# Stick-breaking attention: the scores of four heads stay in four PSUM banks, and the sums of kept logarithms are added onto them by pairs of heads

## The reference

```
z = einsum('bhqd,bhkd->bhqk', q_blk, kh) * scale
mask = (key_pos[None, :] < q_pos[:, None]) & key_valid[None, :]
log_beta = where(mask, log_sigmoid(z), -inf)
log_keep = where(mask, log_sigmoid(-z), 0.0)
later = cumsum(log_keep, axis=3, reverse=True) - log_keep
a = exp(log_beta + later)
out = einsum('bhqk,bhkd->bhqd', a, vh)
```

## Time and profile before

| | us |
|---|---|
| median of 3 runs | 1073.82 |
| lowest and highest | 1071.89, 1075.95 |
| the profiled execution | 1075.32 |
| its span, first to last instruction | 1073.5 |
| PE busy | 1043.0 (97%) |
| DVE, ACT, POOL busy | 596.4, 513.9, 150.2 |
| mean granted clock of TensorE | 0.991 |

### The profile page before, as it was taken

How to read it: one execution, slowest core, us unless ns; L and a number is a source line. 1 busy time by engine, 2 the same in 40 slices (tenths; PEclk the granted TensorE clock), 3 DMA queues, 4 the chain that set the end, 5 groups by cost and what they waited for, 6 DMA issues and landing times.

```text
span 1073.5 us, 20398 instructions
## 1 busy us (share of the span) xinstructions
PE 1043.0 (97%) x7936; PEld 970.1 (90%) x7936; DVE 596.4 (56%) x837; ACT 513.9 (48%) x811; POOL 150.2 (14%) x140
## 2 busy tenths in 40 slices
PE   8899999999989999999989999999999899999998
PEld 5899878889977999999969998788899879999997
DVE  8456345436676555554465564554458666666543
ACT  5442454456445544453455334534563565454542
POOL 2000000000354221110130000000006332212011
PEclk9899999999999999999999999999999999999999
DMA  5673422334442455555525533233354425555551
GB/s 168 228 235 100 147 78 81 118 118 158 145 158 90 157 182 170 169 173 187 168 86 171 183 110 127 79 118 94 128 173 157 157 91 184 195 182 176 195 190 40
DMA packets 156042, 157.46 MB, mean 147 GB/s; under 512 B 6851, under 2 KB 154542, under 8 KB 155598
## 3 DMA queue, kind: packets, MB, share of 16 engines
q1 hardware_dynamic: 155118, 153.17, 44.2%
q10 hardware_dynamic: 672, 3.37, 0.9%
q0 software_dynamic: 192, 0.07, 0.0%
HBM read 155.55 MB, written 1.05 MB: 146 GB/s over the span
## 4 chain that ended last, share of the span: by engine, by line
PE 87%; DVE 8%; ACT 1%; issue 1%; DMA 1%; ACTq 0%; DVEq 0%
PE banks L548 26%; PE banks L550 25%; PE banks L549 25%; DVE sub L1237 2%; DVE xl L1474 2%; DVE term L1481 1%; PE banks L744 1%; DVE sq L1228 1%; PE banks L746 1%; PE banks L573 1%; PE banks L656 1%; DVE lo L1219 1%; DMA raw<-in_w_in 1%; PE banks L772 1%; ACT hi L916 1%
## 5 line engine op out<-in xcount | busy, mean ns | idle before, releaser
L548 PE MATMUL banks<-xh,hi 128*128 128x272 f32 (+1 forms) x1680 | 492.5, 293 | 16.1 <-DVE xl L1252 4.8
L550 PE MATMUL banks<-xh,lo 128*128 128x272 f32 (+1 forms) x1680 | 482.9, 287 | 0.0
L549 PE MATMUL banks<-xl,hi 128*128 128x272 f32 (+1 forms) x1680 | 481.5, 287 | 0.0
L1219 DVE TENSOR_TENSOR lo<-raw,hi 128x1024 fp32r<-128x1024 f32 (+1 forms) x292 | 350.8, 1206 | 182.5 <-ACT hi L916 181.3
L916 ACT ACTIVATE hi<-raw 128x1024 fp32r<-128x1024 f32 (+1 forms) x292 | 302.9, 1041 | 130.1 <-PE banks L550 100.6
L548 PEld LDWEIGHTS banks<-xh,hi 128*128 128x128 f32 x1680 | 319.2, 190 | 31.0 <-issue 14.7
L549 PEld LDWEIGHTS banks<-xl,hi 128*128 128x128 f32 x1680 | 319.0, 190 | 0.7
L550 PEld LDWEIGHTS banks<-xh,lo 128*128 128x128 f32 x1680 | 319.3, 190 | 0.0
L1603 POOL TENSOR_TENSOR half<-term 128x544 f32<-128x544 f32 (+1 forms) x14 | 31.1, 2222 | 518.3 <-DVE term L1481 518.0
L550 PE MATMUL banks<-ah,lo 128*128 128x272 f32 (+1 forms) x352 | 100.4, 285 | 0.0
L548 PE MATMUL banks<-ah,hi 128*128 128x272 f32 (+1 forms) x352 | 100.1, 284 | 0.0
(11 more groups left out here) (239 smaller groups left out, 1094.8 us busy)
## 6 DMA issues: line engine op xcount, KB each, us to landing
raw<-in_w_in SPq DMA_DIRECT2D x60, 1024.0 KB, 5.0
raw<-in_ffn_w_gate SPq DMA_DIRECT2D x22, 1024.0 KB, 5.1
raw<-in_ffn_w_up SPq DMA_DIRECT2D x22, 1024.0 KB, 5.1
raw<-in_ffn_w_down SPq DMA_DIRECT2D x16, 1024.0 KB, 5.2
raw<-in_w_branch SPq DMA_DIRECT2D x8, 1024.0 KB, 5.3
raw<-in_w_out SPq DMA_DIRECT2D x8, 1024.0 KB, 5.2
raw<-in_ffn_w_down SPq DMA_DIRECT2D x8, 768.0 KB, 4.4
const<-in_consts ACTq DMA_DIRECT2D x2, 1042.5 KB, 5.3
```

What stands on the lines that cost most here:

```text
L548: mm(dst, wh, mh, start=start, stop=False)
L549: mm(dst, wh, ml, start=False, stop=False)
L550: return mm(dst, wl, mh, start=False, stop=stop)
L1219: tt(lo[g % 2][:, 0:k, c:c + P], raw[g % 2][:, 0:k, c:c + P], hi[g % 2][:, 0:k, c:c + P].bitcast(F32), ALU.subtract).then_inc(lo_ready, 1)
```

## The change

The score banks are now four, one for each head: `z_banks` = `sc[0]`, `sc[1]`, `ex`, `e0`. All scores are computed once, at the start, and stay there. `sb_exponent` works on a pair of heads and adds the sums onto the scores without computing them again; the sums for the meta keys go onto `k0`, where `sb_scores0` has left its scores. In a score bank only the first matmul has `start`. The softplus, `sb_keep` and `sb_mask` read the bank of their head, `sb_mask0` reads `k0`. The steps are put in another order: both `sb_scores` together; `sb_soft` 1 and `sb_keep` 1 ahead of group `mo`; `sb_soft` 2 and `sb_keep` 2 behind it; `sb_exponent` 0 behind `sbv`; `sb_soft` 3 and `sb_keep` 3 behind that; the second `sb_exponent` behind logit half 0. `gla_scores0` waits in addition for `e0_free`, and `gla_scores` for `ex_free` of all heads. Eight semaphores that existed once for each layer exist once, with a target of l + 1.

```
-           ("sb_scores0",), ("sb_scores", 0), ("sb_soft0",), ("sb_keep0",), ("sb_soft", 0), ("sb_keep", 0),
-           ("group", "mo"), ("sb_exponent", 0), ("sb_soft", 1), ("sb_mask", 0), ("sb_p", 0), ("sb_keep", 1),
-           ("group", "sbv"), ("rest", "sbv"), ("sb_exponent", 1), ("sb_scores", 1)]
+           ("sb_scores0",), ("sb_scores", 0), ("sb_scores", 1), ("sb_soft0",), ("sb_keep0",), ("sb_soft", 0), ("sb_keep", 0),
+           ("sb_soft", 1), ("sb_keep", 1), ("group", "mo"), ("sb_soft", 2), ("sb_keep", 2), ("group", "sbv"), ("rest", "sbv"),
+           ("sb_exponent", 0), ("sb_soft", 3), ("sb_keep", 3)]
...
-    0: [("sb_soft", 2), ("sb_mask", 1), ("sb_p", 1), ("sb_keep", 2)],
-    1: [("sb_soft", 3), ("sb_mask", 2), ("sb_p", 2), ("sb_keep", 3)],
-    2: [("gla_soft",), ("sb_mask", 3), ("sb_mask0",), ("sb_p", 3), ("sb_p0",)],
+    0: [("sb_mask", 0), ("sb_p", 0), ("sb_mask", 1), ("sb_p", 1)],
+    1: [("gla_soft",), ("sb_mask", 2), ("sb_p", 2)],
+    2: [("sb_mask", 3), ("sb_mask0",), ("sb_p", 3), ("sb_p0",)],
...
-    0: [("sb_exponent", 2)],
-    1: [("sb_exponent", 3)],
+    0: [("sb_exponent", 1)],
...
+        z_banks = [*sc, ex, e0]
...
-            def sb_exponent(l, h):
-
-                qs, ks, i, rows = M["sbq"], M["sbk"], h // 2, head_rows[h]
-                keep = M["pt"]
+            def sb_scores(l, i):
+
+                qs, ks = M["sbq"], M["sbk"]
                 pe.wait_ge(rot_free[l], 4)
-                pe.wait_ge(sb_keep0[l], 1)
-                pe.wait_ge(sb_keep[l], h + 1)
-                mm(e0[quad[h], 0:T], ks[rows, i, 0:32], qs[rows, i, :], start=True, stop=False)
-                mm(e0[quad[h], 0:T], cut["negtri0"][quad[h], :], M["pt0"][quad[h], :], start=False, stop=False)
-                mm(e0[quad[h], KB1:T], cut["negones"][:, 0:32], keep[:, h, 0:256], start=False, stop=False)
-                last0 = mm(e0[quad[h], KB2:T], cut["negones"][:, 0:32], keep[:, h, 256:SCW], start=False, stop=True)
-                if h == HEADS - 1:
+                for h in (2 * i, 2 * i + 1):
+                    mm(z_banks[h][:, 0:256], ks[head_rows[h], i, KB1:KB2], qs[head_rows[h], i, KB1:], start=True, stop=False)
+                for h in (2 * i, 2 * i + 1):
+                    mm(z_banks[h][:, 256:SCW], ks[head_rows[h], i, KB2:], qs[head_rows[h], i, KB2:], start=False, stop=True).then_inc(sc_ready[l], 1)
+
+            def sb_exponent(l, i):
+
+                keep, heads = M["pt"], (2 * i, 2 * i + 1)
+                pe.wait_ge(sb_keep0, l + 1)
+                pe.wait_ge(sb_keep[l], 2 * i + 2)
+                for h in heads:
+                    mm(k0[quad[h], 0:T], cut["negtri0"][quad[h], :], M["pt0"][quad[h], :], start=False, stop=False, skip_group_check=True)
+                for h in heads:
+                    mm(k0[quad[h], KB1:T], cut["negones"][:, 0:32], keep[:, h, 0:256], start=False, stop=False, skip_group_check=True)
+                for h in heads:
+                    last0 = mm(k0[quad[h], KB2:T], cut["negones"][:, 0:32], keep[:, h, 256:SCW], start=False, stop=True, skip_group_check=True)
+                if i:
                     last0.then_inc(e0_ready[l], 1)
-                if h:
-                    pe.wait_ge(ex_free[l], h)
-                mm(ex[:, 0:256], ks[rows, i, KB1:KB2], qs[rows, i, KB1:], start=True, stop=False)
-                mm(ex[:, 0:256], cut["negtri"], keep[:, h, 0:256], start=False, stop=False)
-                mm(ex[:, 128:256], cut["negones"], keep[:, h, 256:SCW], start=False, stop=True)
-                mm(ex[:, 256:SCW], ks[rows, i, KB2:], qs[rows, i, KB2:], start=True, stop=False)
-                mm(ex[:, 256:SCW], cut["negtri"], keep[:, h, 256:SCW], start=False, stop=True).then_inc(ex_ready[l], 1)
+                for h in heads:
+                    mm(z_banks[h][:, 0:256], cut["negtri"], keep[:, h, 0:256], start=False, stop=False, skip_group_check=True)
+                    mm(z_banks[h][:, 128:256], cut["negones"], keep[:, h, 256:SCW], start=False, stop=False, skip_group_check=True)
+                    mm(z_banks[h][:, 256:SCW], cut["negtri"], keep[:, h, 256:SCW], start=False, stop=True, skip_group_check=True).then_inc(ex_ready[l], 1)
 
             def gla_scores0(l):
                 d = open_scores0(l, GLA)
+                pe.wait_ge(e0_free[l], 1)
...
             def gla_scores(l, i):
+                pe.wait_ge(ex_free[l], HEADS)
...
             def sb_soft_(l, h):
-                softplus_part(M["sb2"][:, h % 2, :], sc[h % 2][:, 0:SCW], sb_soft[l], 3 * (h + 1), (sc_ready[l], h + 1))
+                if h >= 2:
+                    act.wait_ge(sc_free[l], h - 1)
+                softplus_part(M["sb2"][:, h % 2, :], z_banks[h][:, 0:SCW], sb_soft[l], 3 * (h + 1), (sc_ready[l], h + 1))
```

More of the change, by code:

```diff
@@ L384, in build @@
         sq_first = sem("sq_first")
+        mo_ready, den_abs, hrstd_ready, hlog_ready, sb_p0, sb_keep0, den_ready, ml_em = (
+            sem(n) for n in ("mo_ready", "den_abs", "hrstd_ready", "hlog_ready", "sb_p0", "sb_keep0", "den_ready", "ml_em"))
         names = """
@@ L387, in build @@
             silu_ready silu_scaled rstd_ready xn_ready xh_ready xl_ready post_scaled h_ready pad_set
[L388 to L391, removed]
+            rot_cos rot_done conv_step conv_done gla_soft gla_dve gla_exp gla_ops ml_soft ml_dve
+            sc_ready sc_free ex_ready ex_free k0_ready k0_free e0_ready e0_free sb_soft sb_keep
+            sb_p ml_w o_ready o_free den_dve osq_ready
+            y_step yh_ready yl_ready gates_ready branch_free half_ready merge_step mh_ready
             ml_ready ah_ready al_ready""".split()
@@ L395, in build @@
          pad_set, rot_cos, rot_done, conv_step, conv_done, gla_soft, gla_dve, gla_exp, gla_ops, ml_soft,
-         ml_dve, ml_em, sc_ready, sc_free, ex_ready, ex_free, k0_ready, k0_free, e0_ready, e0_free, sb_soft,
-         sb_keep, sb_keep0, sb_p, sb_p0, ml_w, o_ready, o_free, den_ready, den_abs, den_dve, osq_ready,
-         hlog_ready, hrstd_ready, mo_ready, y_step, yh_ready, yl_ready, gates_ready, branch_free,
+         ml_dve, sc_ready, sc_free, ex_ready, ex_free, k0_ready, k0_free, e0_ready, e0_free, sb_soft,
+         sb_keep, sb_p, ml_w, o_ready, o_free, den_dve, osq_ready,
+         y_step, yh_ready, yl_ready, gates_ready, branch_free,
          half_ready, merge_step, mh_ready, ml_ready, ah_ready, al_ready) = (per_layer(n) for n in names)
@@ L713, in wait_p @@
                 if mix == SB:
-                    pe.wait_ge(sb_p0[l], 1)
+                    pe.wait_ge(sb_p0, l + 1)
                     pe.wait_ge(sb_p[l], h + 1)
@@ L729, in ml_den @@
                     last = mm(e0[0:4, KB2:T], den[:, h, :], M["pt"][:, h, 256:SCW], start=False, stop=h == 3)
-                last.then_inc(den_ready[l], 1)
+                last.then_inc(den_ready, 1)
             def values(l, mix, pair):
@@ L775, in headbc @@
             def headbc(l, p):
-                pe.wait_ge(hrstd_ready[l], 1)
+                pe.wait_ge(hrstd_ready, l + 1)
                 pe.wait_ge(sc_free[l], 4 * HEADS)
@@ L783, in _ @@
                 "group": group, "gate": gate, "rot": rot, "logit": logit, "headsum": headsum, "headbc": headbc,
-                "sb_scores0": sb_scores0, "sb_scores": lambda l, i: scores(l, SB, i, M["sbq"], M["sbk"]),
+                "sb_scores0": sb_scores0, "sb_scores": sb_scores,
                 "sb_exponent": sb_exponent, "gla_scores0": gla_scores0, "gla_scores": gla_scores,
@@ L993, in mo_sigmoid @@
                     wait_taken(act, group_tile(l, "mo") + j)
-                fn(M["mo"][:], M["mo"][:], ACT.Sigmoid).then_inc(mo_ready[l], 1)
+                fn(M["mo"][:], M["mo"][:], ACT.Sigmoid).then_inc(mo_ready, 1)
             def gate_sigmoid(l, n):
@@ L1042, in ml_em_ @@
                 act.wait_ge(ml_dve[l], 11)
-                fn(M["rows"][0:4, 1, :], M["rows"][32:36, 0, :], ACT.Exp, scale=-1.0).then_inc(ml_em[l], 1)
+                fn(M["rows"][0:4, 1, :], M["rows"][32:36, 0, :], ACT.Exp, scale=-1.0).then_inc(ml_em, 1)
             def take_out(l, n):
@@ L1060, in sb_p0_ @@
                 act.wait_ge(e0_free[l], 1)
-                fn(M["pt0"][:], M["cum"][:], ACT.Exp).then_inc(sb_p0[l], 1)
+                fn(M["pt0"][:], M["cum"][:], ACT.Exp).then_inc(sb_p0, 1)
             def ml_w0(l):
@@ L1073, in den_abs_ @@
             def den_abs_(l):
-                act.wait_ge(den_ready[l], 1)
-                act.wait_ge(ml_em[l], 1)
-                fn(M["rows"][0:4, 0, :], e0[0:4, 0:T], ACT.Abs).then_inc(den_abs[l], 1)
+                act.wait_ge(den_ready, l + 1)
+                act.wait_ge(ml_em, l + 1)
+                fn(M["rows"][0:4, 0, :], e0[0:4, 0:T], ACT.Abs).then_inc(den_abs, 1)
             def head_square(l, p):
@@ L1085, in head_rstd @@
                 wait_taken(act, TILE[l][("headsum",)])
-                fn(r, r, ACT.Ln).then_inc(hlog_ready[l], 1)
-                act.wait_ge(hlog_ready[l], 1)
```

(6 more changed lines are left out.)

12 lines of the change are left out of this document (6 added, 6 removed).

## The result

| us | before | with the change |
|---|---|---|
| median | 1073.63 (4 runs) | 1055.34 (4 runs) |
| lowest and highest | 1071.89, 1075.95 | 1053.34, 1055.98 |
| the profiled execution | 1075.32 | 1055.98 |
| its span | 1073.5 | 1054.2 |
| first stick-breaking stage (first meta score matmul to first values matmul) | 46.19 | 36.35 |

The ratio is 0.9825 with a 95% interval from 0.9804 to 0.9845: 1.7% faster. The kernel was forecast at 1053.8 us, in a range from 1050.5 to 1060.

What follows compares the result with a forecast made beforehand. PE, busy 97% of the span, was taken to bound the kernel. Gains of 20.2 us (blocks) and 0.8 (moved scores) less 1.0 (waits) made 20.0 us, from the median 1073.8 to 1053.8 us; range 1050.5 to 1060.

Steps and rivals of the forecast that it cites:

- What bounds: Whole kernel: PE is busy 97% of the span, so a matmul removed in the stick-breaking stage saves its whole spacing.
- The block for two heads: Exponent sums on PE: 3.39 us for two heads instead of 8.44, four times, a gain of 20.2 us.
- Rival A: Exponent blocks: paired matmuls do not overlap, costing 1.16 us a pair, 4.6 us in all; 1058.5 us, chance 8%.
- the Trainium skill's rule: Pairs of `negtri0`: row tiles cannot share a PSUM bank simultaneously, so they run in sequence; 2.0 us, giving 1055.8 us.
- The moved scores: Second pair's scores, now behind the first pair's: 0.65 us instead of 1.03, a gain of 0.8 us in all.
- The new wait: Head of group sbv: PE waits 0.5 us a layer for a lo half behind `sb_keep` 1; 1.0 us in all.
- The two slacks: Third tile of sbv: no wait or 0.1 us; second block, waiting for head 3's keep: 1.7 us to spare.
- The wait for the keep of head 3: Second exponent block: keep ready at 136.4, PE there at 138.1, so hidden with 1.7 us of slack.
- Rival B: Head of sbv, its third tile or the second block: waits of 1 to 2.5 us a layer; 1055.5 to 1059 us, 15%.
- Rival C: Behind the stage: the gain is given back because weights arrive on their own schedule; 1069 to 1075 us, 4%.
- Rival D: Stage waits reach 2.8 us each and PE's clock falls to 1.2 GHz behind them; slower, 1079.5 us, 2%.
- The lower bound of 15 us: Stage's own work on PE: the least saving if no pair overlaps, where 21.0 us was forecast and 21.5 the upper bound.

Runs made afterwards that it cites:

- e1: The change, but in each block all matmuls of one head come before those of the next, instead of by pairs; 1060.29 us, ratio 0.9887.
- e3: The change, but on VectorE the keep of head 1 stands behind the two lo halves of group mo; 1054.20 us, ratio 0.9819.
- e0: The change run again without any edit; 1055.99 us, ratio 0.9845 to the kernel before.
- e7: The change run once more without any edit, on the same chip as e8; 1054.69 us, ratio 0.9829.
- e6: The change with 3.3 us of additional VectorE work in front of the keep of head 1 in each layer; 1061.96 us, ratio 0.9891.
- e8: The kernel of e4 run again, on the same chip as e7; 1051.89 us, ratio 0.9803.
- e4: The change with the keep of head 1 behind group mo's lo halves and that of head 2 behind group sbv's copies; 1050.08 us, ratio 0.9787.

## Why the prediction was right

- **What bounds.** PE, in the stage: what its rows lost the stage lost, less the wait. For one stage 10.0 us was forecast, and 9.84 and 9.83 were measured.
- **The block for two heads** was put at 3.39 us net. It is 3.34 - 0.13 + 0.09 = 3.30. All pairs overlap, as the rows of L650 and L746 said, and of the full-width matmuls a pass over 256 columns takes 0.22 and one over 128 takes 0.11, as taken from L676 and L677. Rival A is out by e1 and by the x4 and x8 rows. With it goes what the Trainium skill's rule ("TensorEngine Tiling (Array Packing)", "Gotcha 1: PSUM Pressure") would have cost here, 0.5 us a block: two and four row groups wrote into bank k0, on different partitions, in 0.65 and 0.66 us beside 0.64 for one. Here the measurement does not agree with the page.
- **The moved scores**: 0.65 us forecast at their new place and 0.65 measured.
- **The new wait** was found at its place and in both layers, but it is 0.74 us from start to start (121.93 - 121.06 = 0.87, less 0.13) and not 0.5. The dates were right; what I left out is the 0.26 us between the end of the lo half and the first matmul behind the wait. So two terms were off and nearly cancelled: 2 x 0.09 = 0.18 us a stage too little gain in the blocks, 0.24 us too little wait. That the stage came out within 0.2 us owes something to this.
- **The two slacks.** At the third tile of sbv I computed none, and found no wait; e3 shows how thin it was, since 0.74 us earlier it was a wait of 0.54. The wait for the keep of head 3 stayed hidden.
- **Rival B** did not come in (it asked for 1 us a layer or more), though its first form is there at 0.74. **Rival C**, the gain given back, is out: between and behind the stages e0 and e7 have the lengths of the kernel before within 0.1 us. **Rival D** asked for waits of 2.8 us. e6 made waits of 4.0 us, and in its trace the mechanism works. At 2.8 us it need not: the one for conv_in was followed by the lower level in the kernel before and in e7, and not in e8, whose window from 31 to 42 us stands at 1.00 above with this wait in it:

```profile
PE banks L550 <- ACT conv_in L979: 2.8, 1, 2.8
```

The forecast was right because the waits in the stage were short, not because the clock would have held behind long ones.
- **The time itself**: 1053.8 us on the median was forecast and 1055.3 measured, 1056.0 and 1054.7 in the repetitions. By the traces the stages give 19.7 us, and the medians have 18.3, 17.0 and 18.0. The missing 1.4 to 2.7 us are no step of the sum, and where they went is open. The profiles do not show it: the first one has 1.5 us more between the stages and 1.2 us less in front of them, and the spans of the three profiles of the change are 19.3, 21.0 and 20.6 us below the one profile of the kernel before, whose execution was itself 1.7 us above its median. The range, 1050.5 to 1060, was wide enough to hold this.
- **Slips in the prediction.** The lower bound of 15 us for the stage's work does not follow from rival A, whose 4.6 us leave 21.0 - 4.6 = 16.4. Rival D's 1079.5 us starts from the profiled execution, 1075.3; from the median it is 1078. Neither touches the forecast.

## What to carry to other kernels

Where the matrix engine is busy without a gap, price a block by the distances from start to start and count the changes of shape: small matmuls of several heads with row or column groups of their own, put one behind the other, cost what one costs, and that was worth as much here as leaving out a third of the matmuls of a head. When steps are moved up in a hand-written order, look on every other engine for the short job that the busy one needs next and that now stands behind a longer one; e4 got the wait back by moving two lines, and moving only one of them just moved the wait. Read differences of 0.2% in the stage of the trace where they arise, not in medians that carry the clock of other parts.

## What was not expected of the hardware

Column groups of 32 with all 128 rows ran four at once: 512 streamed columns for each of four heads, two passes of 256 each, in 0.64 us, beside 0.62 us for one head. A wait of 4.0 us in an otherwise dense stage was followed by 6.8 us at 1.2 GHz in one layer and 3.4 us in the other, while waits of up to 1.5 us mostly, but not always, left the clock alone: the same kernel had stretches near 301 and 332 us in one execution and none there in two others. Nor does it take one long wait: all three traces of the change have 3.4 us at the lower level from 552 or 554 us on, and in the 11 us in front of that PE never waited for more than 0.5 us at a time. The first 3 us of this stretch in e0:

```profile
552.00:555.00 3.00, 3.00 (x14) 3.00 (x15) 2.63 (x7) 0.05 (x1) 0.00 (x0) 0.50 0.03 5
```
